# First weight tile multiplied in whole fp32, its high and low parts made later, and five small products ahead of the first transposes

## The reference, cut to what matters

```
def rms_norm(x, g):
    xf = x.astype(jnp.float32)
    y = xf * lax.rsqrt(jnp.mean(xf * xf, axis=-1, keepdims=True) + EPS)
    return (y * g.astype(jnp.float32)).astype(x.dtype)

h = rms_norm(x, attn_norm)
z = h @ w_in                                     # 256 x 1024 by 1024 x 2852
a_conv, q, kc_r, vc_r, ks, vs, kw, vw, g = jnp.split(z, splits, axis=-1)
u, v = jnp.split(a_conv, 2, axis=-1)             # in conv_mixer: the first two weight tiles
y = u * jax.nn.sigmoid(v)
y = lax.conv_general_dilated(y, w_dw[:, None, :], ..., feature_group_count=CONV_CH) + b_dw   # 31 taps
...                                              # attention, output projection, two feed-forward layers
```

## Time and profile before

| | us |
|---|---|
| median of 3 runs | 759.56 |
| lowest, highest | 758.11, 761.24 |
| the profiled execution: its time | 758.03 |
| the profiled execution: its span in the trace | 756.2 |
| PE busy in the span | 733.1 (97%) |
| DVE busy | 542.4 (72%) |
| ACT busy | 380.9 (50%) |

### The profile page before, as it was taken

One profiled execution on the slowest core, in us unless ns is written; L12 is line 12 of the kernel. 1 busy time (PEld: TensorE's weight loads), 2 busy tenths in 40 slices (PEclk: granted clock), 3 DMA queues, 4 the chain that ended last, 5 costly groups with the idle time before them and its releaser, 6 DMA issues.

```text
span 756.2 us, 13154 instructions
## 1 busy us (share of the span) xinstructions
PE 733.1 (97%) x5308; PEld 676.4 (89%) x5308; DVE 542.4 (72%) x922; ACT 380.9 (50%) x544; POOL 51.2 (7%) x72
## 2 busy tenths in 40 slices
PE   5999998999999999999999999999999999999996
PEld 4999986789999999998999999999978998998995
DVE  6797687587687777766658988785967776555554
ACT  7433767756444333455545347665634544444442
POOL 1950000000000000000333000000000000000000
PEclk9999999999999999999999999999999999999999
DMA  8636411266988878753355456554632675545611
GB/s 333 225 120 224 166 58 57 97 237 247 373 302 332 319 287 320 282 197 112 114 179 176 165 175 242 207 204 182 255 135 76 248 264 192 208 163 184 220 59 56
DMA packets 27022, 151.10 MB, mean 200 GB/s; under 512 B 3128, under 2 KB 7836, under 8 KB 9564
## 3 DMA queue, kind: packets, MB, share of 16 engines
q1 hardware_dynamic: 22620, 124.81, 45.4%
q10 hardware_dynamic: 3456, 25.17, 8.3%
q0 software_dynamic: 896, 0.43, 0.3%
HBM read 148.92 MB, written 1.05 MB: 198 GB/s over the span
## 4 chain that ended last, share of the span: by engine, by line
PE 82%; DVE 11%; ACT 3%; issue 1%; DMA 1%; SPq 0%; DVEq 0%; ACTq 0%
PE ps L464 25%; PE ps L465 24%; PE ps L466 24%; DVE ada L1722 3%; DVE w_lo L1638 2%; PE ps L770 1%; PE ps L595 1%; PE ps L571 1%; DMA raw<-wts 1%; PE ps L1026 1%; ACT w_hi L1203 1%; DVE rows_ga L1768 1%; PE ps L1012 0%; ACT rows_ga L1278 0%; PE ps L1002 0%
## 5 line engine op out<-in xcount | busy, mean ns | idle before, releaser
L1638 DVE TENSOR_TENSOR w_lo<-raw,w_hi 128x2048 fp32r<-128x2048 f32 x106 | 239.9, 2268 | 108.2 <-ACT w_hi L1203 108.1
L464 PE MATMUL ps<-h_hi,w_hi 128*128 128x256 f32 (+2 forms) x1000 | 284.7, 285 | 1.0 <-DVE h_lo L1681 1.0
L465 PE MATMUL ps<-h_lo,w_hi 128*128 128x256 f32 (+2 forms) x1000 | 282.8, 283 | 0.0
L466 PE MATMUL ps<-h_hi,w_lo 128*128 128x256 f32 (+2 forms) x1000 | 282.8, 283 | 0.0
L1203 ACT CAST w_hi<-raw 128x2048 fp32r<-128x2048 f32 x106 | 198.7, 1886 | 50.1 <-PE ps L466 39.4
L464 PEld LDWEIGHTS ps<-h_hi,w_hi 128*128 128x128 f32 (+2 forms) x1000 | 190.2, 190 | 3.4 <-issue 2.3
L465 PEld LDWEIGHTS ps<-h_lo,w_hi 128*128 128x128 f32 (+2 forms) x1000 | 190.2, 190 | 1.2
L466 PEld LDWEIGHTS ps<-h_hi,w_lo 128*128 128x128 f32 (+2 forms) x1000 | 190.2, 190 | 0.3
L464 PE MATMUL ps<-w_hi,mix_hi 128*128 128x512 f32 x248 | 97.5, 393 | 1.2 <-DVE small L1768 0.8
L465 PE MATMUL ps<-w_lo,mix_hi 128*128 128x512 f32 x248 | 96.8, 390 | 0.0
L466 PE MATMUL ps<-w_hi,mix_lo 128*128 128x512 f32 x248 | 96.5, 389 | 0.0
(11 more groups left out here) (302 smaller groups left out, 927.0 us busy)
## 6 DMA issues: line engine op xcount, KB each, us to landing
raw<-wts SPq DMA_DIRECT2D x111, 1024.0 KB, 4.8
ada<-w_ada ACTq DMA_DIRECT2D x24, 1024.0 KB, 5.5
fa_whole<-wts SPq DMA_DIRECT2D x2, 1024.0 KB, 5.7
resid<-x SPq DMA_DIRECT2D x2, 512.0 KB, 4.1
raw<-wts SPq DMA_DIRECT2D x2, 512.0 KB, 6.7
rows_ga<-rows_wide SPq DMA_DIRECT2D x1, 1024.0 KB, 6.9
out<-resid SPq DMA_DIRECT2D x4, 256.0 KB, 2.0
shared<-shared SPq DMA_DIRECT2D x2, 320.0 KB, 6.8
```

The source lines that it names most:

```text
L464: nc.tensor.matmul(o, lh, rh, start=start, stop=False)
L465: nc.tensor.matmul(o, lh, rl, start=False, stop=False)
L466: return nc.tensor.matmul(o, ll, rh, start=False, stop=stop)
L1638: V.tensor_tensor(w_lo[:, s % RING, 0:w], raw[:, n_of[name] % RAW, 0:w], w_hi[:, s % RING, 0:w].bitcast(F32), ALU.subtract).then_inc(w_rea ...
```

## The change

- Tile u is multiplied in whole fp32, straight from `raw`: 16 products (2 halves c by 8 chunks k) of a 128x128 weight chunk by 256 columns, in place of 48. Their values are whole too: ACT writes the eight normed pieces as fp32 into `h_first`, which lies in `fa_whole`, memory that is used only late in the kernel. PE waits for piece k with `first_values_ready`.
- The parts of h are made from `h_first` afterwards, in two lumps of four pieces each: ACT casts 128x1024 to `h_hi` twice, DVE subtracts 128x1024 to `h_lo` twice.
- Tile u gets no high and low part. Tile v, the second, is now the one that is split in halves, behind the lumps of h. PE starts v when the low part of its first half is there, and waits for the second half (`w_ready` 2) at chunk 4.
- SP's load of vc, which goes into u's slot, waits for PE's end of tile u (`pe_tile` 1) instead of `w_ready` 1.
- Five products of the 128x128 identity with itself, into PSUM that nobody reads, stand on PE ahead of the first two transposes. They wait for the identity's transfer alone.

The lines of the diff that say this:

```
             def project_1(s):
-                if s == 0:
+                if s == 1:
                     pe.wait_ge(first_ready, 1)
...
-            for s in range(8):
-                feature_tile(*project_1(s), h_hi, h_lo, 0 if s == 0 else None).then_inc(pe_tile, 1)
+
+            first = raw_of("u").rearrange("p (k c) -> p k c", k=DC)
+            pe.wait_ge(first_landed, 16)
+            for c in range(2):
+                for k in range(DC):
+                    if c == 0:
+                        pe.wait_ge(first_full, k + 1)
+                    if (c, k) == (0, DC // 2):
+                        landed(pe, "u")
+                    i = nc.tensor.matmul(ps[:, 0, c * T:(c + 1) * T], first[:, k, c * P:(c + 1) * P], h_first[:, k, :],
+                                         start=k == 0, stop=k == DC - 1)
+            i.then_inc(pe_tile, 1)
+            for s in range(1, 8):
+                feature_tile(*project_1(s), h_hi, h_lo, 0 if s == 1 else None).then_inc(pe_tile, 1)
...
+            for _ in range(5):
+                nc.tensor.matmul(ps[:, 1, 0:P], ident, ident, start=True, stop=True)
             pe.wait_ge(s_rows, 32)
...
-                    if kind == "s":
+                    if old == "u":
+                        sp.wait_ge(pe_tile, 1)
+                    elif kind == "s":
                         sp.wait_ge(w_ready, s_idx[old] + 1)
...
-            act.wait_ge(first_landed, 16)
-            nc.scalar.copy(w_hi[:, 0, 0:TW // 2], raw[:, 0, 0:TW // 2]).then_inc(first_hi, 1)
-            act.wait_ge(s_raw[0], 16)
-            nc.scalar.copy(w_hi[:, 0, TW // 2:TW], raw[:, 0, TW // 2:TW]).then_inc(hi_ready, 1)
             act.wait_ge(vec_ready, 1)
-            norm_hi(0, lambda k: col("attn_norm", k))
-            for s in range(1, RING):
-                split(s, s_name[s])
+            for k in range(DC):
+                act.wait_ge(xT_ready, k // 2 + 1)
+                src = ps[:, 4 + k // 2, (k % 2) * T:(k % 2 + 1) * T]
+                nc.scalar.activation(h_first[:, k, :], src, ACT.Identity, scale=col("attn_norm", k)).then_inc(first_full, 1)
+            for a in range(2):
+                act.wait_ge(first_full, 4 * a + 4)
+                nc.scalar.copy(h_hi[:, 4 * a:4 * a + 4, :], h_first[:, 4 * a:4 * a + 4, :]).then_inc(hhi_ready, 1)
+            landed(act, "v")
+            nc.scalar.copy(w_hi[:, 1, 0:TW // 2], raw[:, 1, 0:TW // 2]).then_inc(first_hi, 1)
+            nc.scalar.copy(w_hi[:, 1, TW // 2:TW], raw[:, 1, TW // 2:TW]).then_inc(hi_ready, 2)
+            split(2, s_name[2])
...
             def split_half(a, b):
-                return V.tensor_tensor(w_lo[:, 0, a:b], raw[:, 0, a:b], w_hi[:, 0, a:b].bitcast(F32), ALU.subtract)
-
+                return V.tensor_tensor(w_lo[:, 1, a:b], raw[:, 1, a:b], w_hi[:, 1, a:b].bitcast(F32), ALU.subtract)
+
+            for a in range(2):
+                ks = slice(4 * a, 4 * a + 4)
+                dve.wait_ge(hhi_ready, a + 1)
+                V.tensor_tensor(h_lo[:, ks, :], h_first[:, ks, :], h_hi[:, ks, :].bitcast(F32), ALU.subtract).then_inc(h_ready, 4)
             dve.wait_ge(first_hi, 1)
             split_half(0, TW // 2).then_inc(first_ready, 1)
-            dve.wait_ge(hi_ready, 1)
-            split_half(TW // 2, TW).then_inc(w_ready, 1)
+            dve.wait_ge(hi_ready, 2)
+            split_half(TW // 2, TW).then_inc(w_ready, 2)
             dve.wait_ge(vec_ready, 2)
-            norm_lo(0, lambda k: col("attn_norm", k))
-            for s in range(1, RING):
-                split(s, s_name[s])
+            split(2, s_name[2])
```

More of the change, by code:

```diff
@@ L249, in build @@
             "const_landed", "rows_landed", "shared_landed", "w2_landed", "out_written"))
-        s_ident, first_landed, first_hi, first_ready = (sem(n) for n in ("ident_landed", "first_half_landed", "first_half_hi", "first_half_ready"))
+        s_ident, first_landed, first_hi, first_ready = (sem(n) for n in ("ident_landed", "first_half_landed", "v_half_hi", "v_half_ready"))
+        first_full = sem("first_values_ready")
         acc_q2 = sem("acc_quarter2_ps")
@@ L305, in build @@
         x_no = {name: i + 1 for i, name in enumerate(name for kind, name in TILES if kind == "x")}
+        h_first = fa_both[:, 0, :].rearrange("p (k t) -> p k t", k=DC)
         fa_whole = [fa_both[:, i, :] for i in range(2)]
@@ L480, in feature_tile @@
                         if ready == 0 and (c, k) == (0, DC // 2):
-                            pe.wait_ge(w_ready, 1)
+                            pe.wait_ge(w_ready, 2)
                         i = mm3(ps[:, bank, c * T:(c + 1) * T], wh[:, k, cs], wl[:, k, cs], hi[:, k, :], lo[:, k, :],
@@ L1229, in root @@
                 nc.scalar.activation(sqv[:, a:w], msum[:, a:w], ACT.Sqrt).then_inc(sq_ready, 1)
[L1231 to L1235, removed]
             nc.scalar.preload_act_table_set("sqrt_and_others")
@@ L1675, in norm_scale @@
                     V.tensor_scalar(xn[:, m, :], x[:, m, :], rst[:, m:m + 1], None, ALU.mult).then_inc(xn_ready, 1)
[L1677 to L1681, removed]
             def add_out(s, a):
```

## The result

The changed kernel takes 762.3 us (median of 14 runs, 13 of them between 759.7 and 764.1), the kernel before 758.4 in the runs beside it. The ratio is 1.0044 with a 95% interval of [1.0034, 1.0054], so about 3.3 us slower (3.9 by the two medians); the one run of 771.3 us, at a lower clock, is left out of it. The profiled execution takes 762.55 us with a span of 760.8, against 758.03 and 756.2. By the ratio that is inside the 0.5% which I called no change, though the interval excludes no change at all, and the time is above the end of my range, 761.6.

What follows compares the result with a forecast made beforehand. PE, busy 97%, passes the mean earlier only if DVE's line 1735 starts earlier. That start 0.1 us earlier, the longer wait priced at nothing, took profiled 758.03 to 757.9 and the median 759.56 to 759.5 us; range 757.6 to 761.6.

Steps and rivals of the forecast that it cites:

- What bounds the kernel: PE passes the mean, line 645, earlier only if DVE's line 1735 starts earlier; 37.8 us of DVE work follow.
- Values, fp32 products, tile v: Beginning on ACT and PE: first piece 10.35, first product 10.9, 0.438 us each, tile v at about 18.05.
- The sum: Line 1735 at 29.65, 0.1 us earlier; DVE's work unchanged; profiled 758.03 to 757.9, forecast median 759.5.
- vc: SP's load of vc, issued at 18.15 when tile u is done, takes 4.8 us and lands at 22.95.
- q0's landing: q0, issued at 19.25 behind vc, lands 5.0 to 6.3 us later, upper end taken; ACT's cast at 25.5.
- My own condition for being wrong: The prediction is wrong if line 1735 starts before 28.9 or after 30.8.
- a second one: The prediction is wrong if PE waits for a weight tile between 24 and 59 us.
- I price the longer wait at nothing: PE's wait before line 645 grows from 0.9 to about 2.0 us, at no cost to the products behind it.
- The base: Median time of the kernel before, 759.56 us, 1.5 above the profiled execution, from which the forecast started.
- No early clock: Rival: the new identity products don't lift PE's clock early; cast of q0 at 26.4, +0.8 us, 760.3; chance 0.27.
- PE's lead kept: Rival: vc and q0 land early, ACT waits for v only; cast of q0 1.1 us earlier, 758.4; chance 0.19.
- Low clock during tile u: Rival: PE's clock is low through the 16 fp32 products; 7.0 us more for the tile, +7.6 us, 767.2; chance 0.04.

Runs made afterwards that it cites:

- the moved wait alone: Kernel before, with only SP's load of vc waiting for PE's end of tile u instead of u's low part: 762.24 us, ratio 1.0051.
- vc early: Changed kernel, tile u landing in a free half of `fa_both`, so vc is issued once four value pieces are there: 760.31 us, ratio 1.0030.
- the convolution first: Changed kernel, DVE doing u times sigmoid(v) and the first ten taps ahead of q0's low part: 759.71 us, ratio 1.0007.
- with both: Changed kernel, DVE's convolution start ahead of q0's low part and tile u landing in separate memory for an earlier vc load: 756.89 us, ratio 0.9978.
- the products in the wait: Changed kernel plus five plain fp32 products, result unread, ahead of PE's wait for the convolution: 760.28 us, ratio 1.0020.
- the kernel before with the new order: Kernel before, DVE doing u times sigmoid(v) and the first taps ahead of q0's low part: 758.19 us, ratio 0.9987.

## Why the prediction was wrong

**What bounds the kernel: right.** The loss at the mean follows the start of line 1735 (now 1747) as the prediction said. It slipped by 2.4, and DVE needed 69.65 - 32.18 = 37.5 us from there to the end of the taps, where 37.8 was taken. Runs agree by intervention: the moved wait alone loses all, vc early gives part back, the convolution first gives most back, and with both the convolution starts at 25.00 and PE doesn't wait at the mean.

**Values, fp32 products, tile v: right within their cover, each a little late.** First piece 11.09 (10.35 forecast). The sum had the clock rise at 9.4; the transposes of this trace show it at about 10.5 (two stretches of one line; shortest, middle and longest in ns, then first and last start), which is half of the lead assumed, and three other traces with the small products show hardly any lead.

```profile
L532 PE MATMUL ps<-consts,z x5: 273/417/421, 9.9 to 10.7; 128*128 128x128 f32 x5
...
L532 PE MATMUL ps<-consts,z x7: 272/273/273, 10.7 to 11.4; 128*128 128x128 f32 x7
```

First product 11.71 (10.9), 0.438 us a product as taken, tile v at 18.71 (18.05).

**vc: right.** Landed 4.7 us behind its issue (4.8), at 23.65 (22.95); ACT is shown as waiting for it.

**The failed step is q0's landing.** "Between 5.0 and 6.3 us, so 24.25 to 25.55": its issue came at 20.01 and not at 19.25, since v's low part was late, and it took 8.0 us. The upper end was taken from q1 of before, issued 2.4 us behind q0. I took this one row of a queued load for the worst case, but the trace of before has a longer one: vc, issued at 12.69, 4.1 us behind kc's load and with it still in flight:

```profile
raw<-wts SPq DMA_DIRECT2D x1, 1024.0 KB, 7.4
```

With 7.4 the sum would have had q0 at 26.65 and line 1735 an estimated 1 us late. With q0 at 28.0 and not 25.5, line 1735 moves from 29.65 to 32.2, which is what the trace shows. My own condition for being wrong, a start after 30.8, was met. So was a second one, waits of PE for a weight tile between 24 and 59 us:

```profile
48.16 0.39 PE L468 MATMUL ps<-h_hi,w_hi 128*128 128x256 f32 x1 [0.40 <-DVE w_lo L1654]
...
54.47 0.39 PE L468 MATMUL ps<-h_hi,w_hi 128*128 128x256 f32 x1 [0.29 <-DVE w_lo L1654]
```

Around these waits PE loses its lead, and the compressor's first products start at 60.32 against 59.50; as DVE is later still, this costs nothing at the mean. It also means that the wait there, 2.22 us where about 2.0 was worked out, agrees by luck: the 2.0 was 0.9 plus PE's lead of 1.1, while the 2.22 is 0.94 plus the 2.10 by which DVE's taps end later, less the 0.82 by which PE is late itself.

**The second failed step is "I price the longer wait at nothing".** It rested on one row, a wait of 1.69 us at 564.77 followed by products at full pitch. The wait of 2.22 at 67.6 was followed by half clock, 2.7 us in the trace and 1.8 us by the ratios. The prediction looked for a low clock in tile u and had no case for it behind line 645. The range ended 2.1 us above the forecast. Neither step alone passes that: with q0 late and the clock kept the loss is 1.5 us (the products in the wait), and with only the clock lost it would be an estimated 1.8 - 0.1 = 1.7; with both it is 3.3.

The base was off as well, the other way: the forecast stood on 759.56, the median of three runs, where 14 runs of the same kernel give 758.43. That made the miss look 1.1 us smaller than it is.

**Rivals.** No early clock: in the profiled execution it rose a microsecond earlier, in other executions it did not, and its absence costs nothing. PE's lead kept: excluded, ACT waited for transfers. Low clock during tile u: excluded by the pitch, as the 32 records take 7.07 to 7.32 us in all seven traces with the changed beginning. It was less far-fetched than its 0.04 says, though: "the products behind that stall run at the upper level now" rested on one execution, and in the profiled one of the kernel before with the new order they ran at the lower level until 17.2 us. Slower by a late q0, which came about, was missing among them: a q0 later by 1.7 us than the row taken (8.0 against 6.3), or by 0.6 than the longest queued row (7.4), was the mechanism to give the slower side.

## What to carry to other kernels

When a load waits for a slot that is freed later, the loads queued behind it move too: take the landing of the second with the first in flight, from the longest row of a queued load and with room beyond it, and ask which engine's fixed order stands behind it. Where a longer wait of PE is foreseen, price the clock behind it as well (here 1.8 us by the ratios and 2.7 in the trace, behind a wait of 2.2), unless a wait as long, after the same kind of work, is seen to leave it up. And where an engine works in a written order, ask what in front of the work that bounds the end could stand behind it: in the kernel before, that alone gained about 1 us (0.2 to 1.9), where the change lost 3.3.

## What the runs showed of the hardware

- At the mean, right behind 7.3 us of 66-column products, waits of PE of 1.43 (convolution first), 1.65 (vc early), 2.04 (without the small products), 2.22 and 2.23 us were followed by the lower clock; with vc early it fell only 1.3 us or more after PE had gone on. One of 0.94 at the same place was not, nor one of 1.69 elsewhere. Length alone doesn't decide; what else does, these runs don't show.
- A low clock can cost nothing. The kernel before has a granted clock of 0.50 of its own from 94 us, with no wait of PE ahead of it, behind 48 products of 16 columns (90.14 to 93.2 us); the changed kernel has the same products and 1.00 behind them. But PE next waits for ACT there, less long (0.49 us, where the changed kernel waits 1.87), so the distance between the two kernels stays what it was:

```profile
94.00:96.00 2.00, 2.00 (x11) 2.00 (x11) 1.83 (x7) 1.99 (x6) 0.00 (x0) 0.50 0.03 8
```

- A load of 1 MB alone takes 4.7 us. In five traces one issued 0.8 to 1.3 us behind another takes 7.8 to 8.8, in the kernel with the moved wait alone one issued 0.37 us behind takes 9.1 and the one ahead of it 7.0. Where nothing else was in flight (q1 held back), the last 2 us of it had a mean DMA share below 0.1. "DMA: Bandwidth & Descriptors" in the Trainium skill says in Queues, rings and completion order that a copy is split over up to 16 engines' rings, and in Why a DMA increments its semaphore by 16 and not by 1 that only the full count means that all data has landed. The trace agrees as far as it goes: at a share of 0.04 to 0.08 ACT's cast still waits.
- A plain fp32 product of 256 columns leaves two records and takes 0.438 us, as worked out from line 770's rows; 16 of them took 7.07 to 7.32 us in seven traces.
